# One maximum over both key ranges, sinks as three columns, and the whole rotation on VectorE, in a four-layer diffusion step

## The reference

```python
def rope_2d(x, cos, sin):
    ...
    out = jnp.stack([a * c - b * s, a * s + b * c], axis=-1).reshape(x.shape)
...
        s_ctx = jnp.einsum('bqhgd,bkhd->bhgqk', qn, k_ctx, preferred_element_type=F32) * scale
        s_loc = jnp.einsum('bqhgd,bkhd->bhgqk', qn, kw, preferred_element_type=F32) * scale
        s_loc = jnp.where(m, s_loc, NEG_INF)
        s_sink = jnp.broadcast_to(sink_b, s_ctx.shape[:-1] + (1,))
        p = jax.nn.softmax(jnp.concatenate([s_ctx, s_loc, s_sink], axis=-1), axis=-1).astype(v.dtype)
```

## Time and profile before

| | |
|---|---|
| median of 3 runs | 4102.17 us (4098.21 to 4104.33) |
| the profiled execution as a run | 4102.17 us |
| its span in the profile | 4100.4 us |
| mean granted clock of TensorE | 0.986 |
| TensorE busy | 3897.5 us, 95% |
| VectorE, ScalarE, GpSimd busy | 2737.5, 2362.8, 1233.5 us |
| attention with a sink, first to last sink product | 2449.8 to 2883.4 us |

### The profile page before, as it was taken

One profiled execution on the slowest core, in us unless ns is written; L12 is line 12 of the kernel. 1 busy time (PEld: TensorE's weight loads), 2 busy tenths in 40 slices (PEclk: granted clock), 3 DMA queues, 4 the chain that ended last, 5 costly groups with the idle time before them and its releaser, 6 DMA issues. The chain is left out here.

```text
span 4100.4 us, 58246 instructions
## 1 busy us (share of the span) xinstructions
PE 3897.5 (95%) x20892; PEld 1932.6 (47%) x20892; DVE 2737.5 (67%) x3695; ACT 2362.8 (58%) x3099; POOL 1233.5 (30%) x868
## 2 busy tenths in 40 slices
PE   6999999999999999999999988888999999999998
PEld 3544444444455544444455554444455444444444
DVE  6346777777449378888755438888553667777754
ACT  5434777777435267787732237778333457777761
POOL 0010334444313124454522113333210114444443
PEclk9999999999999999999999999999999999999999
DMA  6238222222102432222112433332111552222111
GB/s 237 67 104 234 69 67 68 69 65 54 65 31 79 129 93 57 68 57 61 27 65 73 120 109 76 84 83 57 61 46 69 164 160 52 52 44 54 42 50 53
DMA packets 376195, 329.44 MB, mean 80 GB/s; under 512 B 247632, under 2 KB 295312, under 8 KB 374448
## 3 DMA queue, kind: packets, MB, share of 16 engines
q1 hardware_dynamic: 375984, 326.60, 28.6%
HBM read 235.30 MB, written 91.23 MB: 80 GB/s over the span
## 5 line engine op out<-in xcount | busy, mean ns | idle before, releaser
L1963 DVE TENSOR_REDUCE max_parts<-bank 128x1 f32<-128x512 f32 (+2 forms) x1536 | 963.4, 648 | 256.0 <-PE bank L1918 233.8
L786 PE MATMUL bank<-H_hilo,w_hilo 128*128 128x512 f16 (+1 forms) x5760 | 1048.0, 345 | 16.2 <-DVE w_hilo L1038 7.5
L2204 ACT ACTIVATE p_f<-bank 128x1024 f32<-128x1024 f32 (+2 forms) x768 | 741.7, 966 | 507.3 <-PE bank L2150 463.7
L2150 PE MATMUL bank<-q_slots,k_slots 96*128 96x512 f16 (+7 forms) x3968 | 942.3, 367 | 6.1 <-PEq L1208 3.1
L2271 DVE TENSOR_TENSOR p_lo<-p_f,p_hi 128x1024 f16<-128x1024 f32 (+2 forms) x624 | 757.4, 1217 | 155.7 <-ACT p_hi L2208 151.6
L786 PEld LDWEIGHTS bank<-H_hilo,w_hilo 128*128 128x128 f16 x5760 | 564.2, 98 | 499.9 <-issue 13.1
L2208 ACT ACTIVATE p_hi<-bank 128x1024 f16<-128x1024 f32 (+2 forms) x768 | 737.6, 960 | 0.0
L1918 PE MATMUL bank<-k_slots,q_slots 96*128 96x512 f16 (+4 forms) x1536 | 525.3, 370 | 71.2 <-DVE max_parts L1963 58.7
L2150 PEld LDWEIGHTS bank<-q_slots,k_slots 96*128 96x128 f16 (+2 forms) x3968 | 371.7, 99 | 401.1 <-issue 31.1
L2340 POOL TENSOR_TENSOR p_lo<-p_f,p_hi 128x1024 f16<-128x1024 f32 x144 | 315.4, 2190 | 571.7 <-ACT p_hi L2208 547.9
L2322 POOL TENSOR_TENSOR o_gated<-o_f,gate_rows 64x512 f32<-64x512 f32 (+1 forms) x192 | 227.2, 1183 | 830.3 <-DVE o_f L2251 625.5
(11 more groups left out here) (205 smaller groups left out, 3909.8 us busy)
## 6 DMA issues: line engine op xcount, KB each, us to landing
ada_w<-in_w_ada SPq DMA_DIRECT2D x48, 768.0 KB, 5.4
gate<-z_ring SPq DMA_DIRECT2D x32, 640.0 KB, 3.3
gate_rows<-gate SPq DMA_DIRECT2D x64, 320.0 KB, 3.9
q_slots<-q_mla SPq DMA_DIRECT2D x64, 240.0 KB, 3.1
k_mla<-H_hilo SPq DMA_DIRECT2D x64, 224.0 KB, 3.2
k_slots<-k_mla SPq DMA_DIRECT2D x64, 224.0 KB, 4.4
cq_hilo<-v_scratch SPq DMA_DIRECT2D x64, 224.0 KB, 3.3
w_f<-in_mla_in SPq DMA_DIRECT2D x24, 512.0 KB, 3.8
```

The costliest lines, as they stand in the source:

```text
L786: ins = pe.matmul(dst, lhs(a, k), rhs(b, k), start=(k == 0 and n == 0), stop=(k == nk - 1 and n == 2))
L1963: dve.tensor_reduce(mx[:, par, t, c:c + 1], MB[(b * NE + k) % 2][:, 0:n], AX.X, ALU.max).then_inc(s_red.h, 1)
L2150: ins = pe.matmul(dst, lhs, rhs, start=(m == 0), stop=(m == len(ops) - 1), skip_group_check=swa)
L2204: act.activation(p32[:, p % 2, 0:cols], src, ACT.Exp, scale=scale).then_inc(s_p32.h, 1)
```

## The change

1. In the layer with a sink a latent tile is one entry: the 512 cached keys go to one bank of the pair `MB`, the window to the other, and one reduction reads both (896 or 768 columns, the second range beginning behind the 512 of the first). The two context tiles are one entry. There are 13 entries a head instead of 22; one of them fills both banks, and the next waits until it is reduced. The order of entries over steps is written out by hand; turns go to a part of a score bank that its step leaves free, and the scores that come into this bank two steps later wait for the copy.
2. The sink's exponentials are taken before the turn, over 128 partitions x 4 columns; the negated maximum and the two halves of the exponential are three columns that are transposed together and copied as three rows of the queries, and the sink product reads these rows.
3. VectorE makes the sine products too, in `project` and in `middle`; in `middle` the second group's sum and output come a turn later.
4. The constant for the sink product is set by two memsets in the first stage.

```diff
@@ start
-                dve.tensor_copy(self.c16[32:33, 4], cf[0:1, 4]).then_inc(s_c16.h, 1)
+                dve.memset(self.c16[HD:HD + 3, 4, HD:P], 1.0).then_inc(s_c16.h, 1)
+                dve.wait_ge(s_c16.h, s_c16.base + 3)
+                dve.memset(self.c16[HD:HD + 1, 4, HD:P], 0.0).then_inc(s_c16.h, 1)
@@ project
-                            if above_zero(g["after"]["pool"]):
-                                dve.wait_ge(s_pr.h, s_pr.base + g["after"]["pool"])
...
-                    pool.tensor_tensor(vv, zs(g["tiles"][-1]), self.sin[:], ALU.mult)
-                    pool.tensor_tensor(y, zs(g["tiles"][0]), self.sin[:], ALU.mult).then_inc(s_pr.h, 1)
+                        dve.tensor_tensor(vv[0:n], zb, self.sin[rb], ALU.mult)
+                        link(dve.tensor_tensor(y[0:n], za, self.sin[ra], ALU.mult))
@@ middle
-        s2, s2b, s3 = {2: 0, 4: 1}, {3: 0, 5: 1}, {4: 0, 6: 1}
+        turns_cos, turns_sin, turns_sum, turns_out = {2: 0, 4: 1}, {3: 0, 5: 1}, {3: 0, 6: 1}, {4: 0, 7: 1}
...
+                    if t in turns_sin:
+                        g = turns_sin[t]
+                        if above_zero(g):
+                            dve.wait_ge(s_st2.h, s_st2.base + g)
+                        dve.tensor_tensor(vv, z[:, 2 * g + 1], self.sin[:], ALU.mult)
+                        dve.tensor_tensor(y, z[:, 2 * g], self.sin[:], ALU.mult).then_inc(s_d.h, 1)
@@ attention
-                    found.append(("max", u, t, 0, 0, 512, []))
-                    found.append(("max", u, t, 1, PAST + lo * P, (hi - lo + 1) * P, masks))
+                    found.append(("max", u, t, 0, PAST + lo * P, (hi - lo + 1) * P, masks))
...
+            entries = c_ + a_[:3] + [("turn", 2)] + a_[3:] + b_[:3] + [("turn", 0)] + b_[3:]
...
+        early = [1, 1, 1, 1, 0, 0, 1, 2, 1] if swa else [1] * (NS - 1) + [0]
...
+            for k, j in enumerate([0, 1, 2, 2, 3, 3, 4, 5, 6, 7, 7, 8, 8]):
+                at_step[j].append(k)
...
+                    first_k, first_n = (k0, n) if u == 2 else (0, PAST)
+                    pe.matmul(MB[0][:, 0:first_n], Q[0:kk, q_slot(hd, b), 0, q0:q0 + P],
+                              K[0:kk, k_slot(hd, b), 0, first_k:first_k + first_n], start=True, stop=True)
+                    q0 += P if u == 2 else 0
+                    mb = MB[1]
...
+                if swa:
+                    pe.wait_ge(s_el.h, s_el.base + hd * 3 + nturn[k] + 1)
...
+                if u == 2:
+                    dve.tensor_reduce(m4[:, par, 0:nt], bank[2][:, :, 0:n], AX.X, ALU.max).then_inc(s_red.h, 1)
+                else:
+                    dve.tensor_reduce(m4[:, par, t:t + 1], both[:, 0:PAST + n], AX.X, ALU.max).then_inc(s_red.h, 1)
...
+                act.activation(es32[:, par, 0:nt], negm[:, par, 0:nt, 0], ACT.Exp, scale=scale * MAX_UNIT,
+                               bias=sink[:, at(hd)]).then_inc(s_es.h, 1)
+                act.activation(negm[:, par, 0:nt, 1], negm[:, par, 0:nt, 0], ACT.Exp, scale=scale * MAX_UNIT,
+                               bias=sink[:, at(hd)]).then_inc(s_eh.h, 1)
...
+                self.wait_gates(dve)
                 dve.tensor_scalar(sink_raw[:], sink, 1.0 / scale, None, ALU.mult).then_inc(s_raw.h, 1)
...
+        at_tile = [3, 3, 4, 5, 5, 6, 7, 7, 8, 8, 9, 10, 10] if swa else [3 + k * 2 // 5 for k in range(NE)]
...
+                            if (p - 2) % NS in turned_in and 0 <= head < HEADS - 1:
+                                pe.wait_ge(s_mr.h, s_mr.base + (head + 1) * 3 + turned_in[(p - 2) % NS] + 1)
```

More of the change, by code:

```diff
@@ L885, in project @@
             g["rows"] = g["rope"][0].stop if rope else P
-            if rope and g["rows"] == P:
-                cum["pool"] += 1
             g["nsrc"] = 2 if rope else len(g["tiles"])
@@ L1100, in _ @@
                         dve.tensor_tensor(ob[0:n, 0], za, self.cos[ra], ALU.mult)
[L1101 to L1121 removed]
+                        dve.tensor_tensor(ob[0:n, 1], zb, self.cos[rb], ALU.mult)
+                        if above_zero(g["vy_free"]):
+                            dve.wait_ge(s_st2.h, s_st2.base + g["vy_free"])
+                        dve.tensor_tensor(vv[0:n], zb, self.sin[rb], ALU.mult)
+                        link(dve.tensor_tensor(y[0:n], za, self.sin[ra], ALU.mult))
             @block.tensor
@@ L1786, in attention, with entry_bank @@
         turn_order = {e[1]: nturn[k] for k, e in enumerate(entries) if e[0] == "turn"}
-        parts = {0: 2 if swa else 3, 1: 2 if swa else 3, 2: 1}
+        parts = {0: 1 if swa else 3, 1: 1 if swa else 3, 2: 1}
         first_step = 2 if mla else 0
-        early = [1] * (NS - 1) + [0]
+        early = [1, 1, 1, 1, 0, 0, 1, 2, 1] if swa else [1] * (NS - 1) + [0]
         at_step = {j: [] for j in range(NS)}
-        for k in range(NE - 1):
-            at_step[first_step + k * (NS - 1 - first_step) // (NE - 1)].append(k)
-        at_step[NS - 1].append(NE - 1)
+        if swa:
+            for k, j in enumerate([0, 1, 2, 2, 3, 3, 4, 5, 6, 7, 7, 8, 8]):
+                at_step[j].append(k)
+        else:
+            for k in range(NE - 1):
+                at_step[first_step + k * (NS - 1 - first_step) // (NE - 1)].append(k)
+            at_step[NS - 1].append(NE - 1)
+        step_of = {k: j for j in range(NS) for k in at_step[j]}
+        turned_in = {step_of[k]: nturn[k] for k in range(NE) if swa and entries[k][0] == "turn"}
+        both = bank[2][:].rearrange("p b n -> p (b n)")
+        def entry_bank(b, k):
+            if not swa:
+                return MB[(b * NE + k) % 2]
+            if entries[k][0] != "turn":
+                return MB[0]
+            return SB[((1 - b) * NS + step_of[k]) % 2][:, 1]
         P2 = 2 * NS
@@ L1893, in emit_entry @@
         def emit_entry(pe, hd, b, k):
-            mb = MB[(b * NE + k) % 2]
+            mb = entry_bank(b, k)
             j = k - 2
+            if swa:
+                j = k - 1
+                while entries[j][0] == "turn":
+                    j -= 1
             hh, jj = (hd, j) if j >= 0 else (hd - 1, j + NE)
-            if not (isinstance(hh, int) and hh < 0):
+            if not (isinstance(hh, int) and hh < 0) and not (swa and entries[k][0] == "turn"):
                 if entries[jj][0] == "max":
@@ L1977, in sink_lo @@
+        unit_of = {o: u for u, o in turn_order.items()}
+        sink_exp_at = {0: 0, 6: 1, 10: 2}
+        sink_lo_at = {2: 0, 7: 1, 11: 2}
         def sink_lo(dve, hd, b, o):
-            q0, nq = units[next(u for u in range(3) if turn_order[u] == o)]
+            par, nt = (3 * b + o) % 2, units[unit_of[o]][1] // P
             dve.wait_ge(s_eh.h, s_eh.base + hd * 3 + o + 1)
-            dve.tensor_tensor(erow[32:33, b, q0:q0 + nq], es_row[o], erow[0:1, b, q0:q0 + nq], ALU.subtract
+            dve.tensor_tensor(negm[:, par, 0:nt, 2], es32[:, par, 0:nt], negm[:, par, 0:nt, 1], ALU.subtract
@@ L1994, in copy_rows @@
+            if e[0] != "turn":
+                return
+            q0, nq = units[e[1]]
+            r = entry_bank(b, k).bitcast(F16)
             act.wait_ge(s_me.h, s_me.base + hd * NE + k + 1)
[L1995 removed]
+            act.activation(Q[mrow:mrow + turned, q_slot(hd, b), 0 if mla else 1, q0:q0 + nq], r[0:turned, 0:nq], ACT.Copy
                            ).then_inc(s_mr.h, 1)
[L1997 to L2000 removed]
@@ L2276, in body @@
                             take_entry(dve, i * 2 + b + 1, 1 - b, k)
-                        if swa and p < P2:
-                            for o in ((0, 1), (2,))[p % NS] if p % NS < 2 else ():
-                                sink_lo(dve, i * 2 + b, b, o)
                         if mla:
@@ L2372, in attention @@
         s_pp.done(NB * so_far(P2 - 1, True))
-        s_row.done(2 + swa); s_me.done(HEADS * NE); s_red.done(HEADS * NM)
-        for s in (s_m4, s_neg, s_mr, s_lnd, s_rd, s_o, s_og, s_oh, s_ol):
+        s_row.done(2); s_me.done(HEADS * NE); s_red.done(HEADS * NM)
+        s_m4.done(0 if swa else 3 * HEADS)
+        for s in (s_neg, s_mr, s_lnd, s_rd, s_o, s_og, s_oh, s_ol):
             s.done(3 * HEADS)
```

153 lines of the change are left out of this document (64 added, 89 removed).

## The result

The changed kernel takes 4037.19 us (median of 4 runs, 4034.25 to 4043.57), the kernel before 4102.66 in the same session: a ratio of 0.9847 (95% interval 0.9834 to 0.9859), 65.5 us less. The forecast was 4049, a gain of 53. Its profiled execution took 4035.7 us between its ends, before 4100.4.

A forecast was written before the change was run, and what follows sets the result against it. TensorE, busy 95% of the span, was taken as the bound, so only its waits give time: 39 + 3 + 3 + 8 = 53 us off 4102 makes 4049 us, own range 4023 to 4082, stated range 4018 to 4086.

The forecast's parts named there:

- The bound: Attention with a sink: only TensorE's waits can give time back; TensorE becomes the fullest engine, at least 22.0 us a head.
- The maxima: Attention with a sink: merged entries cut VectorE's reductions from 10.5 to 9.05 us a head, 1.08 us for 896 columns.
- rival (a): Attention with a sink: half of each of eight reductions shows, 27.8 us a head, 4085 us in all; chance 0.12.
- The sink: Attention with a sink: small exponentials cost 1.0 us a head instead of 3.6, subtractions 0.5 instead of 1.8.
- bound of 0.35: Attention with a sink: upper end in us for each of ScalarE's six small exponentials, 2.1 a head.
- What is lost: Attention with a sink: 1.5 us of waits and 1.8 of collisions with GpSimd make 25.4 us a head, saving 39 us.
- walk of 23.6 us: Attention with a sink: a head's nine steps followed with the forecast's prices, 1.5 us of waits and no collision in it.
- rival (b): Collisions fall into slack and the slow clock goes: 23.3 us a head, higher ends elsewhere, 4012 us; chance 0.11.
- (c): Attention with a sink: whole reduction and drain show at each of nine entries, 33.2 us a head, 4166 us; chance 0.04.
- (d): Waits only get another releaser and the rotation's stall moves to turn 7: within 8 us of before; chance 0.05.
- The change of block and the values: Ahead of the attention with a sink: row exponentials leave the chain's end, saving 3 us, bounds 0 and 5.
- The rotation: All products on VectorE: saves 3 us in the second layer's projection, 4 in each of two makings of queries.

## Why the prediction was right, and where it was off

**The bound.** Right: places where TensorE waits gave the time, and it is now the fullest engine. The floor was wrong. I counted columns and got 22.0 us a head; the busy time of the earlier trace rows already said 24.2, and the run with half the low halves gives 24.2. The sum had a slip too: at its own price of 0.22 us for 512 columns the 50,700 columns are 21.8 us, and with the 0.9 of small products 22.7. And a count of columns leaves out what lies at each change of kind. On the timeline of TensorE after:

```profile
2608.50 0.27 PE L2147 MATMUL bank<-p_lo,v_hi_ones 128*128 128x256 f16 x1
2608.70 0.28 PE L2150 MATMUL bank<-q_slots,const_f 3*128 3x256 f16 x1
2608.91 0.50 PE L2176 MATMUL bank<-q_slots,k_slots 128*128 128x384 f16 x2
```

Products of 256 columns follow each other by 0.11 us, but here by 0.20 and 0.21. Six such products and turns a head are about 1 us of the 2. The slip is another 0.3, by the 0.216 us from product to product that the trace has for 512 columns; the rest I didn't trace.

**The maxima.** Right: 896 columns cost 1.084 us (1.08 forecast) and 768 cost 0.953 (0.95). A reduction over both banks is on the line of the three sizes of the earlier trace rows. With one entry in flight TensorE waits for maxima once in 14 heads, so rival (a) is out: it wanted half of each reduction to show. (The upper end of this term was 10.3 us a head by its prices, 6 x 1.24 + 2 x 1.11 + 0.68, and not 10.0.)

**The sink.** ScalarE's small exponentials take 0.298 and 0.291 us, not 0.17; two on each other's heels take 0.5 us (0.19 from start to start), 1.4 a head and not 1.0. This is near the bound of 0.35, which the forecast named as a sign of being wrong, and it did no harm: 2.4 us a head more on ScalarE cost only 1.8 us in the whole stage. The small subtraction takes 0.363 instead of 0.165 (0.15 alone, 0.57 while GpSimd works). VectorE has 21.5 us a head (20.6 forecast), ScalarE 20.2 (19.7).

**What is lost, the term that was mis-sized.** 25.4 us a head was forecast and 25.0 is the measure (bounds 24.3 to 26.8), and over 15 heads and what lies at the ends -39 became -47.8. Three errors stand in it. First, the low halves were to meet GpSimd for 2.7 us a head, 1.8 of them on TensorE's path. In the changed kernel the longest takes 1.70 us and not 2.14, and TensorE waits for them 0.3 us a head. Between 2500 and 2790 us all low halves together lose 1.0 us a head beside GpSimd, in the kernel before 1.5. It isn't that fewer stand beside GpSimd: they overlap with it for 4.7 us a head, before for 3.7. A low half that starts while an instruction of GpSimd runs takes longer by what is left of that instruction, less some 0.13 us: 2.14 us with 1.06 left, 1.43 with 0.35 left. Here a reduction, which isn't slowed, stands in front, and the low half comes near the end of GpSimd's multiplication. VectorE at one output:

```profile
2610.83 1.08 DVE L1978 TENSOR_REDUCE max_rows<-bank 128x1 f32<-128x896 f32 x1
2611.83 1.43 DVE L2297 TENSOR_TENSOR p_lo<-p_f,p_hi 128x1024 f16<-128x1024 f32 x1
```

GpSimd beside it:

```profile
2610.91 1.26 POOL L2345 TENSOR_TENSOR o_gated<-o_f,gate_rows 64x512 f32<-64x512 f32 x1 [6.75 <-DVE o_f L2277]
```

Second, and against this, the walk of 23.6 us rested on columns and was too short by the floor's error of 2.0. The two errors nearly cancel in the head, so that 25.4 came close to the measure is in part luck. Third, a head before was 28.3 us and not 28.0: 14 heads that gave back 3.2 each are 45 of the 47.8 us, the first and the last share the rest. The full overlap of rival (b), 23.3, can't be had: it lies below TensorE's work. Rivals (c) and (d) didn't come; VectorE isn't a step behind, and of the old waits only 4.4 us came back, as waits for outputs.

**The change of block and the values.** -3 was forecast, +0.2 came. The row exponentials did leave the end of the chain, but the last maximum, the small exponentials and the subtraction came into it:

```profile
2421.49 0.38 PE L1953 MATMUL bank<-const_f,neg_max 128*3 128x128 f16 x4 [2.98 <-DVE neg_max L2002]
2424.51 1.86 PE L2176 MATMUL bank<-q_slots,k_slots 128*128 128x512 f16 x4 [2.63 <-PEq L1189]
```

That chain was costed at 2.3 us and stands with 2.98, and the change of block with 2.63 instead of 2.20; what I had down as given back, the waits for several maxima, was 4.3 us before and is 2.2 after (0.79 and 1.44). The wait for stored gates on VectorE cost 0.8 us: the scaling of the sinks behind it takes 3.13 us, where it took 0.17, and the first low half of the values comes late. It starts at 2385.96, and beside it, from 2385.98, runs a memset of GpSimd of 3.08 us that waited for the same gates. The forecast had this wait at 0, or 1 if not.

**The rotation.** The mechanism was right: products of 1.48 us with no 4.19 among them. The page SBUF — State Buffer of the Trainium skill (Who interferes with whom) says that an instruction of VectorE with two inputs in SBUF contends with one of GpSimd that reads SBUF; the trace agrees, with 4.19 us beside GpSimd's product and 1.48 without it. The projection's gain was mis-sized, -5.7 for -3. The forecast shortened only the last group's chain. In the traces the last group begins 2.0 us earlier in the stage, since the groups ahead of it are shorter too, and from its first product to its last low half VectorE takes 19.7 us for 22.6. Most of the 2.9 is one split of weights, which stood beside GpSimd's second sine product and now takes 1.23:

```profile
1345.86 3.80 DVE L1038 SCALAR_TENSOR_TENSOR w_hilo<-w_f,w_hilo 128x1024 f16<-128x1024 f32 x1
```

Together 4.9 us, more than the stall, and with it goes the slow clock behind it:

```profile
1374.00:1379.00 5.00, 4.86 (x16) 1.98 (x17) 2.45 (x2) 3.14 (x5) 0.00 (x0) 0.68 0.64 262
```

(a stretch of the kernel before; 0.32 of 5 us is 1.6). In the making of queries the stall at turn 7 was forecast at 3.1 us and 42.8 us into the stage; it is 2.99 us at 46. The 4.50, 1.46 and 1.80 of the earlier trace rows are gone. -4 each became -5.8 and -6.0. The forecast's own sum gave 4.7 or 7.1, and it took less without a reason. The clock did fall behind the new stall, but it cost 1.5 us and not 2.4, which makes 10.2 - 4.5 = 5.7.

**The rest.** The +3.7 us of the first stages can't be put down to a part of the change. In the fourteen traces the first making of queries starts at 247.3 to 252.7 us, and the kernel before is the earliest: the six with the old attention lie at 247.3 to 250.4, the eight with the new entries at 249.4 to 252.7. But two kernels with the same lines up to there, the rotation alone and the merged entries with rows, start it at 249.3 and 252.5. The first stage's waits for modulation weights differ from trace to trace, and 1.7 us of the 3.7 are the clock's (the last section). Whether the change adds something to this isn't shown.

The -2.7 at the end is one wait. For split weights of the last products TensorE stood 2.14 us before, with 32.94 us for the 144 products behind it, and stands 1.08 after, with 31.25: 1.1 us, and 1.7 of the clock. This wait is 2.14 to 2.52 us in the six traces with the old attention and 0.7 to 1.6 in the eight with the new entries; by what path they reach it isn't shown. These 2.7 us less and the 3.7 more at the start, both forecast at 0, nearly cancel in the total, which is luck.

**The sums.** The range from the ends of the terms comes to 4021 to 4080 (22 and 81 us), not 4023 to 4082, and rival (b) with the higher ends elsewhere (25 us, not 20) to 4007. Neither touches the reading of the result.

## What to carry to other kernels

Take the floor of an engine from its busy time in a tight stretch, not from a count of columns. When three engines are close, ask of an added or removed instruction what it shifts the next ones onto: the row subtractions cost half as much again as they took, since they moved the start of a low half behind that of an instruction of GpSimd. And test two reliefs of one engine together before making both: here each alone gave 38 to 43 us, both 48.

## What the runs showed of the hardware

A reduction on VectorE that reads the matmul banks isn't slowed by GpSimd: the 84 over 896 columns take 1070 to 1093 ns, as the line through the smaller sizes gives, and about half of them overlap with GpSimd's work.

Between a low half (two inputs in SBUF) and an instruction of GpSimd the one that starts first keeps its time, and the other waits for it, but for one kind of case. In 51 low halves between 2500 and 2790 us, before and after, that started with 0.2 us or more of GpSimd's instruction left, the added time was what was left less 0.12 to 0.14 us (1.06 left, 0.93 added; 0.62 and 0.49; 0.35 and 0.22). The other way round GpSimd pays: its subtraction of 1.15 us took 1.95 where a low half had started 0.14 us before it.

```profile
2601.76 1.08 DVE L2271 TENSOR_TENSOR p_lo<-p_f,p_hi 128x896 f16<-128x896 f32 x1
```

```profile
2601.90 1.95 POOL L2328 TENSOR_TENSOR H_hilo<-o_gated,H_hilo 64x512 f16<-64x512 f32 x1
```

Five in the kernel before don't fit: there a cast of GpSimd began 0.13 us ahead of the low half and took 1.45 us for 0.40, and the low half lost nothing.

The same stall doesn't always cost the same. With the rotation changed in the making of queries alone TensorE stands the same 2.99 us at turn 7, and the 90 products behind it take 15.76 us; in the changed kernel they take 17.29. The stretches of 5 us, first of the former, then of the latter:

```profile
295.00:300.00 5.00, 5.00 (x30) 2.74 (x29) 2.48 (x6) 1.59 (x4) 0.00 (x0) 1.00 0.64 192
```

```profile
295.00:300.00 5.00, 2.95 (x12) 1.80 (x13) 4.65 (x8) 2.72 (x8) 0.00 (x0) 0.68 0.55 156
```

The granted clock stayed at 1.00 (2.4 GHz) in one and fell toward 1.2 GHz in the other. The kernel doesn't decide it: of fourteen such stalls of 2.99 or 3.00 us, in both layers of seven kernels, twelve had 17.05 to 17.44 us behind them and two 15.76, and in both of these kernels the other layer's stall was dear. Nor does the length alone. The first layer's projection has a stall of 1.75 to 2.25 us at its start in all fourteen traces: in six of them (1.75, 1.86, 1.94, 2.01, 2.03 and 2.18 us) the next 216 products took 39.10 us, in eight (1.99 to 2.25) they took 40.79. In the second layer 72 products behind a stall of 2.06 us took 14.83 us and behind 2.03 us 13.14. What decides it, these runs don't show. Such a stall cost 1.5 to 1.7 us on top in some traces and nothing in others, and a difference of that size between two kernels need not be the change's.
